# First projection unit split between memory copies, tile 6 transposed ahead of the first projection bank and tile 7 ahead of the second

## What is computed

```
h = rmsnorm(x, g_mix_pre[l])
z = h @ w_in[l]
q, k, v, u, qx, gates = jnp.split(z, _IN_SPLITS, axis=-1)
...
mkv = rmsnorm(mem, g_mem[l]) @ w_mem_kv[l]
km, vm = jnp.split(mkv, 2, axis=-1)
...
y_mem = memory_cross_attention(qx, km, vm)
...
x = x + rmsnorm(merged @ w_out[l], g_mix_post[l])
h = rmsnorm(x, g_mlp_pre[l])
f = jnp.square(jax.nn.relu(h @ w_up[l])) @ w_down[l]
x = x + rmsnorm(f, g_mlp_post[l])
```

## Time and profile before

| | us |
|---|---|
| median of 3 runs | 1575.19 |
| lowest and highest of them | 1572.78, 1575.23 |
| the profiled execution | 1576.14 |
| its span in the trace | 1574.4 |
| PE busy, share of the span | 98% |
| DVE busy, share of the span | 52% |
| ACT busy, share of the span | 29% |
| mean granted TensorE clock | 0.995 |

### The profile page before, as it was taken

How to read it: one execution, slowest core, us unless ns; L and a number is a source line. 1 busy time by engine, 2 the same in 40 slices (tenths; PEclk the granted TensorE clock), 3 DMA queues, 4 the chain that set the end, 5 groups by cost and what they waited for, 6 DMA issues and landing times.

```text
span 1574.4 us, 18626 instructions
## 1 busy us (share of the span) xinstructions
PE 1542.2 (98%) x7531; PEld 1286.9 (82%) x7531; DVE 815.2 (52%) x1558; ACT 453.1 (29%) x641; POOL 114.9 (7%) x181
## 2 busy tenths in 40 slices
PE   7899999999999999999999999999999999999997
PEld 6688779878888888888888888888888888888886
DVE  5558658647745725446767543333333333333348
ACT  4243734232132344211334312112120212122132
POOL 0000010041220221000000200000000000000000
PEclk9899999999999999999999999999999999999999
DMA  8301121242113255224423320111111111101104
GB/s 321 67 27 54 36 92 34 81 134 94 68 54 101 61 191 181 84 96 158 148 94 99 129 80 28 53 53 53 53 34 46 53 53 53 53 27 53 54 0 174
DMA packets 82209, 130.95 MB, mean 83 GB/s; under 512 B 13120, under 2 KB 55136, under 8 KB 82144
## 3 DMA queue, kind: packets, MB, share of 16 engines
q1 hardware_dynamic: 67696, 80.75, 15.5%
q0 software_dynamic: 14448, 49.31, 9.0%
HBM read 104.88 MB, written 25.17 MB: 83 GB/s over the span
## 4 chain that ended last, share of the span: by engine, by line
PE 96%; DVE 3%; ACT 1%; issue 0%; DMA 0%; DVEq 0%; SPq 0%; ACTq 0%
PE bank L1449 87%; PE bank L1459 3%; PE bank L1485 2%; PE bank L1681 1%; PE bank L1569 1%; PE bank L1637 1%; PE bank L1696 1%; PE bank L1701 1%; PE bank L1665 0%; PE bank L1584 0%; DVE prob L1023 0%; DVE mx L1021 0%; DVE wlo L325 0%; DVE tok L1421 0%; DMA xst<-in_mem_dram 0%
## 5 line engine op out<-in xcount | busy, mean ns | idle before, releaser
L1449 PE MATMUL bank<-hThi,whi 128*128 128x512 f32 x1184 | 464.7, 392 | 7.1 <-DVE wlo L325 4.8
L1449 PE MATMUL bank<-hTlo,whi 128*128 128x512 f32 x1184 | 462.3, 390 | 0.0
L1449 PE MATMUL bank<-hThi,wlo 128*128 128x512 f32 x1184 | 462.1, 390 | 0.0
L1449 PEld LDWEIGHTS bank<-hThi,whi 128*128 128x128 f32 x1184 | 223.0, 188 | 55.2 <-issue 9.1
L1449 PEld LDWEIGHTS bank<-hThi,wlo 128*128 128x128 f32 x1184 | 223.2, 189 | 46.6
L1449 PEld LDWEIGHTS bank<-hTlo,whi 128*128 128x128 f32 x1184 | 223.3, 189 | 45.9
L319 ACT ACTIVATE whi<-raw 128x2048 fp32r<-128x2048 f32 x61 | 116.3, 1910 | 365.8 <-PE bank L1449 333.5
L1449 PE MATMUL bank<-whi,yhi 128*128 128x512 f32 x512 | 199.3, 389 | 0.8 <-DVE wlo L325 0.8
L1449 PE MATMUL bank<-wlo,yhi 128*128 128x512 f32 x512 | 199.2, 389 | 0.0
L1449 PE MATMUL bank<-whi,ylo 128*128 128x512 f32 x512 | 199.2, 389 | 0.0
L325 DVE TENSOR_TENSOR wlo<-raw,whi 128x2048 fp32r<-128x2048 f32 x61 | 139.7, 2292 | 68.4 <-ACT whi L319 68.2
(11 more groups left out here) (306 smaller groups left out, 1720.4 us busy)
## 6 DMA issues: line engine op xcount, KB each, us to landing
raw<-in_w_in_dram SPq DMA_DIRECT2D x34, 512.0 KB, 4.6
raw<-in_w_up_dram SPq DMA_DIRECT2D x32, 512.0 KB, 4.3
raw<-in_w_down_dram SPq DMA_DIRECT2D x32, 512.0 KB, 4.3
gate_scratch<-scr POOLq DMA_DIRECT2D x48, 256.0 KB, 2.3
tok<-gate_scratch POOLq DMA_DIRECT2D x24, 512.0 KB, 3.6
y_scratch<-yst POOLq DMA_DIRECT2D x16, 256.0 KB, 2.4
yst<-y_scratch POOLq DMA_DIRECT2D x16, 256.0 KB, 4.2
raw<-in_w_out_dram SPq DMA_DIRECT2D x8, 512.0 KB, 4.4
```

The source lines that it names most:

```text
L1449: ins = T.matmul(dst, lhs(k)[p], rhs(k)[q], start=start and k == 0 and i == 0, stop=stop and k == kt - 1 and i == 2)
```

## The change

It moves four things and adds or removes none.

- ACT: `prep_hi(U_QX)` moves up to stand between `norm_hi(6)` and the copy of `memory(3, 0)`. `norm_hi(8)` and `norm_hi(9)` stand ahead of the copies of banks 0 and 1 of the unit.
- DVE: `prep_lo(U_QX)` moves from ahead of `norm_h(9)` to behind `norm_h(8)`, ahead of `norm_lo(7)`. `norm_lo(8)` moves ahead of `prep_lo(U_QX + 1)`.
- PE: the transposes of `idx` 8 come before bank 0 (and before the wait for the unit), those of `idx` 9 before bank 1.
- The numbers of the bank uses follow: `norm_event(8, e)` from 25, 26 to 24, 25, `norm_event(9, e)` from 28, 29 to 27, 28, `qx_event(0, 0)` from 24 to 26, and `qx_event(0, 1)` from 27 to 29.

```diff
@@ norm_event, qx_event
-    return (2 * idx if idx < 2 else 3 * idx if idx < 8 else 3 * idx + 1) + e
+    return (2 if idx < 2 else 3) * idx + e
...
-    return 32 + m if s else 24 + 3 * m if m < 2 else 28 + m
+    return 32 + m if s else 26 + 3 * m if m < 2 else 28 + m
@@ ACT
                     norm_hi(2 * s + i)
                     if s < 3:
                         square(4 + 2 * s + i)
+                    elif i == 0:
+                        prep_hi(act, U_QX, None)
                     memory(s, i)
-            prep_hi(act, U_QX, None)
             prep_hi(act, U_QX + 1, None)
             for m in range(2):
+                norm_hi(8 + m)
                 copy_out(qx_event(0, m), tokq[:, m, 0:512])
-                norm_hi(8 + m)
@@ DVE
                 norm_lo(idx - 2)
-                if idx == 9:
+                norm_h(idx)
+                if idx == 8:
                     prep_lo(dve, U_QX)
-                norm_h(idx)
+            norm_lo(8)
             prep_lo(dve, U_QX + 1)
-            norm_lo(8)
             norm_lo(9)
@@ PE
-            unit(U_QX)
             for m in range(2):
+                norm_transposes(8 + m)
+                if m == 0:
+                    unit(U_QX)
                 project_half(m)
-                norm_transposes(8 + m)
```

## The result

| | before | changed |
|---|---|---|
| median, first comparison (4 runs each) | 1575.21 us | 1565.09 us |
| lowest and highest | 1572.78, 1575.89 | 1563.30, 1566.01 |
| ratio of the runs, 95% interval | | 0.9937 (0.9920 to 0.9954) |
| span of the profiled execution | 1574.4 us | 1561.5 us |
| mean granted TensorE clock | 0.995 | 0.998 |

The changed kernel is 10.1 us faster by the medians; 1564.3 was forecast, with 1561.5 to 1568.9 as the range.

The account below looks back on a forecast made before the run. PE, busy for 98% of the span, was taken as the bound. 4.78 + 2.46 + 1.82 + 1.81 = 10.9 us took the profiled 1576.14 to 1565.3; 0.95 less gave the median forecast 1564.3 us, range 1561.5 to 1568.9.

Parts of the forecast that it names:

- The two pauses: PE's waits at the first projection unit, 4.78 us for `wlo` and 1.82 us for `hTlo`, would both go entirely.
- The cover on ACT, DVE and the queues: Moved work fits idle time or finishes before PE needs it; the position load and arithmetic stay covered, the latter by 5.9 us.
- The first half-clock stretch: First projection bank behind the 4.78 us pause: 7.93 us instead of 5.47 at full clock; the 2.46 us would go.
- The second half-clock stretch: Two projection banks behind the 1.82 us pause: 12.75 us instead of 10.94 at full clock; the 1.81 us would go.
- The rule of the Trainium skill: Clock falls only behind gaps clearly longer than 1.82 us, so the later projection stretch would stay: 9.1 us gained.
- theory A: From the experiments: a 1.8 us pause lowers the clock only sometimes, by when it falls; about a third to two thirds of 14.
- The size of the scatter: Whole-kernel runs of before lie within 2.45 us, so the range starts 2.8 us below the forecast.
- a half-clock stretch stays: Rival at the projection: half clock remains without the pauses; gain 9.1 us (1566.1) or 6.6 us (1568.6); chance 0.13.
- the wait moves: Rival at the first projection unit: early `whi` does not come early, PE idles 3.9 us; 4.5 us gained, 1570.7; chance 0.03.
- the gain is given back: Rival: a later engine, only DVE in the score stage a candidate, binds; no change, 1575; chance 0.03.
- the clock falls ahead of the scores: Rival: half clock behind the pause ahead of the scores makes it 8.5 us slower, 1583.7; chance 0.02.

Follow-up runs that it names:

- k = 2: Changed kernel with PE waiting ahead of bank 2 until ACT, after two extra unread copies, has copied bank 1: 1567.27 us (4 runs).
- k = 4: Changed kernel with PE waiting ahead of bank 2 until ACT, after four extra unread copies, has copied bank 1: 1569.61 us (6 runs).

## Why the prediction was right, and where it was not

**The two pauses** (4.78 and 1.82 us): right. Both rows are gone from the waits, and each part alone removes what it should: the early `wlo` leaves the 1.8 us, the new order leaves 3.7 of the 4.8, of which the transposes fill 0.87.

**The cover on ACT, DVE and the queues**: right, to a few tenths once the 1.6 us of the start are taken off. `whi` leaves ACT 1.01 us (1.0 forecast), `wlo` is ready 3.4 us early (3.4), `idx` 9 is taken at 57.0 (58.7 - 1.6 = 57.1; by its own terms, 57.11 + 1.48, the 58.7 should have been 58.6), and the position arithmetic ends at 66.2 (67.9 - 1.6 = 66.3). The position load now shares the DMA engines: 4.9 us to landing for 3.2, and nobody waits for it.

**The first half-clock stretch** (2.46 us): right in kind. It stood behind the pause in every profile that had the pause, and in none without. Its size depends on the execution: 2.46, 2.79 and, with the shorter pause of the new order alone, 2.80 us.

**The second half-clock stretch** (1.81 us): the term of the sum that was not what I took it for. The step that failed is "the second begins 1.4 us after the end of the 1.82 us idle", read as the work of a pause of 1.82 us that comes every time. Three profiles have this pause behind the eight transposes, and only the first, from which I forecast, has the stretch. The pause of 1.86 us between matmuls (k = 2) had full clock behind it, and so had all 28 of 1.57 to 1.66 us. The size was a little off too. Behind the same pause two banks at full clock take 11.12 to 11.16 us and not 2 x 5.47 = 10.94, so about 1.6 us of the 1.81 are clock and 0.2 belong to the pause.

So before paid for this stretch in some executions, and the change is worth, in the length used above, 10.9 us against the one profile of before and 9.6 (55.49 - 45.85) against the other. The medians say 10.1 and 11.1. The forecast of 10.9 took all of it as certain; 9.3 plus a share of 1.6 would have been the better term. That 10.9 came so near to both medians is in part luck.

The rule of the Trainium skill that I set against this row (TensorE: Matmul & The Clock Gate, section on HAM oscillation) did better than my reading for the short pauses. By it the clock falls only behind longer gaps, and the traces agree with that at both ends: 0 of 29 between matmuls at 1.57 to 1.86 us, 17 of 17 at 3.7 us and over. They do not agree in between, where the 2.8 us pause and once the 1.82 us pause, both shorter than the gap that the page names, had half clock behind them. I had also read the rule to mean that the second half-clock stretch would stay after the change, and it did not.

What sets the cases apart is open. The two profiles of before come from one program, with the same pauses to 0.01 us, and only one has the second stretch; so neither the length of the pause nor what the program does ahead of it can be the whole cause. What is left is when in an execution the pause falls, which is theory A, and the six runs of k = 4 would fit it. No run here varies that on purpose for a pause of 1.82 us.

The eight transposes ahead of the pause (0.87 us) were an obvious suspect: with them PE is without a common matmul for 2.7 us, close to the pause of 2.8 us. The same page says of transposes (Part 4, PE-mode transpose) that they do not count as PE being busy in the same way. The traces speak against it here. Two of the three profiles with the same transposes and the same pause kept full clock. And at the start of the changed kernel PE has done nothing but 16 transposes, at half speed (3.59 us), when the memory products begin at full clock: 7.14 us for 32, as in four other profiles. So in this kernel transposes were enough to bring the clock up.

**The size of the scatter** was taken from before's runs, 2.45 us. A part of it will be the half-clock stretch at the start: the first 32 memory products took from 7.14 to 9.44 us in the profiles.

**The rivals.** That a half-clock stretch stays, that the wait moves, that the gain is given back and that the clock falls ahead of the scores are all ruled out by the profile after.

## What to carry to other kernels

When one engine is busy for 98% of the span, look for the few pauses it has and for the slow matmuls behind them: here 6.6 us of pauses cost up to some 4 us more in half clock. Work that needs only data already there (the split of a loaded weight) belongs into idle time of its engines ahead of the last thing that the busy engine waits for. Before a clock stretch goes into a sum as certain, profile the kernel a second time, or put the same pause, at its full length, into one run many times.

## What the runs showed of the hardware

- TensorE's clock and pauses of PE: full clock behind all 28 pauses of 1.57 to 1.66 us between matmuls and behind one of 1.86; behind a pause of 1.82 us with eight transposes ahead, half clock in one profile of three. Half clock behind one of 2.8 us, and behind all 17 of 3.7 to 7.6 us, for 3.0 to 5.7 us after the pause.
- Transposes alone can bring the clock up: in five profiles the memory products, behind 16 transposes at half speed and 1.0 us idle, run at full clock from the first on (7.14 us for 32). In seven others the clock rises only within them (8.7 to 9.4 us).
- At the start, the windows grant 1.00 where matmuls are still at half speed: in the changed kernel 10 to 15 us shows 1.00, and its 16 transposes took 3.59 us where two sets of eight take 2 x 0.87 later. There the durations tell the clock, and the granted clock does not.
- Products of `ident` with itself were enough to bring the clock up: behind them the transposes took 0.11 us each from the first on, not 0.22.
